# Two fused transformer blocks in fp32 on one core: five changes of order, and a gate projection spread 1, 2, 2, 2 instead of 1, 3, 2, 1

## What is computed

```python
xn = rms_norm(x, norm_gain)
qa, ka, va, za, qi, ki, wi, qb, kb, vb, zb = split(xn @ w_in)     # 8 heads of 64 in each half
a_out = dsa_attention(...)      # an index score picks the 128 keys of each query (top-k), softmax over them
b_out = dilated_attention(...)  # three dilated windows
x = x + concat([a_out * silu(za), b_out * silu(zb)]) @ w_out
...
x = x + hybrid_layer(x, ...)    # second block: compressed, selected and window attention, pooling
x = x + square(relu(rms_norm(x) @ w_ff1)) @ w_ff2
return rms_norm(x)
```

## Time and profile before

| | before |
|---|---|
| median of three runs | 1025.14 us (1024.88 to 1025.60) |
| the profiled execution | 1025.67 us, its span 1023.7 us |
| PE busy | 1007.1 us, 98% of the span |
| DVE, ACT, POOL busy | 66%, 54%, 41% |
| PE clock granted | 0.999 of full |

### The profile page before, as it was taken

How to read it: one execution, slowest core, us unless ns; L and a number is a source line. 1 busy time by engine, 2 the same in 40 slices (tenths; PEclk the granted TensorE clock), 3 DMA queues, 4 the chain that set the end, 5 groups by cost and what they waited for, 6 DMA issues and landing times. The chain is left out here.

```text
span 1023.7 us, 14244 instructions
## 1 busy us (share of the span) xinstructions
PE 1007.1 (98%) x5158; PEld 828.0 (81%) x5158; DVE 678.5 (66%) x1201; ACT 555.2 (54%) x1013; POOL 422.4 (41%) x403
## 2 busy tenths in 40 slices
PE   9999999999999999999999999999999999999997
PEld 7788877778778898878887778888888888888885
DVE  5578898788975256733577879344332225999997
ACT  7455354777862456544667874224443346554555
POOL 0024012666730003900354520007779965774753
PEclk9999999999999999999999999999999999999999
DMA  9533321337140384132200461249999941443552
GB/s 338 104 98 98 98 62 42 83 84 203 46 175 1 122 278 133 46 99 62 63 2 1 156 209 47 83 143 306 361 350 338 349 166 63 153 152 126 209 183 82
DMA packets 100165, 146.24 MB, mean 143 GB/s; under 512 B 6480, under 2 KB 60496, under 8 KB 100096
## 3 DMA queue, kind: packets, MB, share of 16 engines
q1 hardware_dynamic: 86800, 130.75, 39.0%
q10 hardware_dynamic: 12768, 12.88, 4.0%
q0 software_dynamic: 528, 1.70, 1.0%
HBM read 123.69 MB, written 21.63 MB: 142 GB/s over the span
## 5 line engine op out<-in xcount | busy, mean ns | idle before, releaser
L2653 DVE TENSOR_TENSOR w_lo<-wring,w_hi 128x1024 fp32r<-128x1024 f32 x32 | 50.6, 1583 | 108.2 <-ACT w_hi L1997 108.2
L2144 DVE TENSOR_TENSOR u_lo<-wring,u_hi 128x1024 fp32r<-128x1024 f32 (+2 forms) x69 | 83.4, 1215 | 53.2 <-ACT u_hi L1650 52.5
L966 PE MATMUL bank<-u_hi,h_hi 128*128 128x512 f32 (+1 forms) x288 | 110.9, 385 | 0.1
L966 PE MATMUL bank<-u_hi,h_lo 128*128 128x512 f32 (+1 forms) x288 | 109.2, 379 | 0.0
L966 PE MATMUL bank<-u_lo,h_hi 128*128 128x512 f32 (+1 forms) x288 | 109.0, 378 | 0.0
L966 PE MATMUL bank<-h_hi,w_hi 128*128 128x512 f32 (+2 forms) x272 | 103.2, 379 | 0.0
L1650 ACT ACTIVATE u_hi<-wring 128x1024 fp32r<-128x1024 f32 (+1 forms) x64 | 66.2, 1034 | 68.2 <-PE bank L966 51.3
L966 PE MATMUL bank<-h_hi,w_lo 128*128 128x512 f32 (+2 forms) x272 | 103.1, 379 | 0.0
L966 PE MATMUL bank<-h_lo,w_hi 128*128 128x512 f32 (+2 forms) x272 | 103.1, 379 | 0.0
L966 PE MATMUL bank<-h_hi,u_hi 128*128 128x512 f32 x224 | 93.4, 417 | 0.4 <-ACT arena L1592 0.2
L1478 PE MATMUL bank<-s_hi,f_hi 128*128 128x512 f32 x224 | 87.5, 391 | 1.1 <-DVE f_lo L2687 0.9
(11 more groups left out here) (400 smaller groups left out, 2598.8 us busy)
## 6 DMA issues: line engine op xcount, KB each, us to landing
wring<-in_w_in SPq DMA_DIRECT2D x60, 512.0 KB, 3.9
wring<-in_w_ff ACTq DMA_DIRECT2D x12, 1024.0 KB, 9.0
wring<-sums_kept SPq DMA_DIRECT2D x16, 768.0 KB, 4.2
wring<-in_w_ff SPq DMA_DIRECT2D x22, 512.0 KB, 6.6
wring<-in_w_ff SPq DMA_DIRECT2D x32, 256.0 KB, 3.3
sums_kept<-wring SPq DMA_DIRECT2D x22, 256.0 KB, 5.1
wring<-in_w_out SPq DMA_DIRECT2D x2, 2048.0 KB, 13.0
wring<-in_w_ff SPq DMA_DIRECT2D x4, 1024.0 KB, 6.9
```

The lines of the kernel that those rows point to most:

```text
L966: last = mm(b, lhs, rhs, start=(start and n == 0), stop=(stop and n == 2))
L2144: done = v.tensor_tensor(u_lo[raw_place(u)][:, cols], raw_unit(u)[:, cols], u_hi[hi_place(u)][:, cols].bitcast(F32), ALU.subtract)
L2653: v.tensor_tensor(cut(w_lo[ring3(m)]), src, cut(w_hi[ring3(m)]).bitcast(F32), ALU.subtract).then_inc(w_lo_done, 1)
```

## The change

Six edits, none of which adds or removes an instruction.

```diff
-    FILL_STEPS = 4 * ((0, 2, 2, 3, 4, 5, 6),) + 3 * ((0, 1, 2, 2, 3, 3, 4, 5, 6, 7),) + ((0, 1, 2, 2, 3, 3),)
+    FILL_STEPS = 4 * ((0, 2, 3, 4, 5, 6, 7),) + 3 * ((0, 1, 2, 2, 3, 3, 4, 5, 6, 7),) + ((0, 1, 2, 2, 3, 3),)
...
@@ tensor: the held products
                 for t in range(2):
                     second_of(m, 0, t)
+                if m > held[0]:
+                    second_of(held[0], 1, m - held[1])
...
             for q in (1, 2):
                 for t in range(2):
-                    for m in held:
+                    for m in held[1 if q == 1 else 0:]:
                         last = second_of(m, q, t)
...
@@ scalar: after the attention loop
-            mixed_high(7, slice(0, S // 2))
             for m in (8, 9):
                 wo_high(m)
+            mixed_high(7, slice(0, S // 2))
             low_rows_of(GROUPS - 1)
...
@@ vector: projections
                 for k in range(3):
-                    if g != "va":
-                        low(unit_of[(g, k)] + HI_UNITS)
                     if done is not None and k > 0:
                         head_low(done, 2 * k - 2)
                         head_low(done, 2 * k - 1)
+                    if g != "va":
+                        low(unit_of[(g, k)] + HI_UNITS)
                     search(counts[k + 1])
...
@@ vector: attention loop
+            def gate_work(t):
+                if t in MIX_LOW_AT:
+                    mixed_low(MIX_LOW_AT[t])
+                if t in GATED_LATE:
+                    gated(FILL1[GATED_LATE[t]])
...
-                if t == NS + 2:
-                    collect1(GROUPS - 2)
...
-                if t in MIX_LOW_AT:
-                    mixed_low(MIX_LOW_AT[t])
-                if t in GATED_LATE:
-                    gated(FILL1[GATED_LATE[t]])
+                if t < NS - 2:
+                    gate_work(t)
...
+                if t == NS - 2:
+                    gate_work(t)
                 if t == NS:
                     mix(6)
+            collect1(GROUPS - 2)
             mix(7, slice(0, S // 2))
```

## The result

| | before | changed |
|---|---|---|
| median of 22 runs each, same chip | 1025.34 us (1024.72 to 1025.97) | 1026.43 us (1025.31 to 1030.30) |
| ratio | | 1.0016, 95% interval 1.0010 to 1.0022 |
| the profiled execution | 1025.67 us, span 1023.7 us | 1025.31 us, span 1023.3 us |

The changed kernel is slower by 1.1 us, 0.16%. The forecast was 1022.7 us, with a range up to 1024.9: the time lies 1.5 us above the range. The slowdown is smaller than the 0.2% that the prediction took as the least that can be told, but the interval of this timing leaves out 1. Rival 1 (every stall pays) is furthest off.

What follows compares the result with a forecast made beforehand. PE was taken as the bound, busy 1007.1 of 1023.7 us, so gains lay in single waits. Terms 1.5 + 0 + 0.9 + 0 = 2.4 us off 1025.14 gave 1022.7 us, range 1020.5 to 1024.9.

Steps and rivals of the forecast that it cites:

- Rival 1: Every stall removed pays, the tail's 1.1 and 140's 0.8 us on top: 1020.8 us; chance 15%.
- spread of the chunks: First four head pairs: moving a gate chunk from iteration 2 to 6 removes 2.3 us of waits, adds 0.5 and 0.3.
- head_low ahead of low: PE's 0.64 us stall at 140 goes, gaining 0.8 us, but PE waits 0.8 us longer at va: gain 0.
- steps 62 to 66, wo_high: At 283 to 297 us both edits give 1.5 us, of which 0.9 survives the weight units' DMA-anchored chain at 308.
- held products: At 1005 us two products fill PE's 0.94 us stall; PE ends 1.4 us sooner, but DVE sets the end: gain 0.
- sign that the prediction named for being right: No idle at head pair starts or 140, waits near step 4, va and L1015, POOL scaling 0.7 us, PE ending 1.4 earlier.
- I take 0.3 us of new wait: Head pair 3: PE would arrive at 211.4, DVE's score of step 27 end at 211.6 to 212.0, costing 0.3 us.
- Rival 2: The spread only shifts waits, as iteration 4 of each pair becomes the place to wait: 1024.2 us; chance 20%.
- A backlog ... holds the same instructions in either order: DVE's top-k rounds from 128.1 us delay head_sum regardless of the edit, so PE still waits at va.
- to make it up: From 102 to 128 us DVE's 3.1 us idle would absorb about 0.4 us lost in each of four slots.
- moves up only 0.5 us (0.8 less 0.3): Step 63's last transpose, behind which SP issues the weight DMAs, comes 0.5 us sooner after late reciprocals cost 0.3.
- keeps its wait for `f_lo`: In the tail, the banks of q = 0 that start DVE's chain stay unmoved, so the held products gain 0.

Runs made afterwards that it cites:

- The three timings: The changed kernel timed three times against the kernel before: 1026.43 beside 1025.34 us, 1026.07 beside 1025.60, 1026.41 beside 1025.25.
- the third profile: Profile from the third timing of the unaltered changed kernel, whose median was 1026.41 us beside 1025.25 of before, ratio 1.0010.
- the version that beats both: Kernel before with spread in head pairs 1 to 3, low parts first, head_low in qa, one search round moved, 62-66 and wo_high edits, no held products: 1023.00 us, 0.9980.
- the moved round: Changed kernel with one top-k search round moved from the last slot of qa to the first of va: PE 1.4 us better than the changed kernel at 152.
- the last version: The 1023.00 us version with late_half ahead of collect1 and mix, product 12's high part earlier, one unit low part ahead of DVE's first addition: 1022.71 us, ratio 0.9980.
- the repeats: The kernel before, unchanged, executed three more times for its profile: all end 0.72 to 0.75 us sooner behind 998 than its first profile.
- the kernel with the pair first: Kernel before with the spread, and DVE making steps 18 and 19's low part first in iteration 22: PE gains 0.18 us from 152 to 222; execution 1029.06 us.

## Why the prediction was wrong, by its steps

| term | forecast, us gained | measured | where |
|---|---|---|---|
| spread of the chunks | 1.5 (0 to 2.3) | -0.22 to -0.27 | head pair 3 gives all back |
| head_low ahead of low | 0 (up to 0.8) | -0.24 to -0.31 | collision at 97 and 102 |
| steps 62 to 66, wo_high | 0.9 (0.45 to 1.5) | +0.31 to -0.66 | units asked for no sooner, and landing late |
| held products | 0 (0 to 1.1) | -0.38, or 0 in the slower pattern | q = 0 comes later |
| sum | 2.4 | -0.5 to -1.6 | -0.22 -0.24 +0.31 -0.38, -0.27 -0.31 -0.66 -0.38 |

The three timings, -1.09, -0.47 and -1.16 us, lie in or at the edge of the last line. The profiles come out lower than two of the timings: from 50 us to the end of the span the changed kernel's three took 0.55 us more in the mean than the four of before.

Nearly every sign that the prediction named for being right was seen: no wait before L1119 at the starts of head pairs and 0.43 us at a step 4, none at 140 and 1.11 at va, POOL's scaling in 0.66 us, PE's last product ending 1.5 us before DVE's last add. The wait at L1015 stood where the earlier trace rows has these transposes, not at 304 to 305, and only the third profile shows it as idle time (0.96 us). The signs told whether the waits aimed at would go, and none of them looked for a new one in head pair 3 or at the transposes of step 63. (Two thirds of 0.60 and 0.15 are 0.55, not 0.57.)

**The spread: the step that failed is "I take 0.3 us of new wait" in head pair 3, and the 0.5 of gain behind it.** Of the waits named, those of 179.59 and 192.98 went as forecast, and the one at step 4 of head pair 0 came with 0.44 us where 0.5 was said. The one of 220.41 went too, where PE came 0.2 us later. Head pairs 1 and 2 gained 0.77, where the prediction's waits add up to 0.97. But the wait of 0.35 us at 209.16, which was to go, grew to 1.07. I had looked at the scores of step 27 for the new wait and not at what stands on DVE ahead of the low part in iteration 22, and I took DVE's durations as fixed. The wait at step 28 itself was sized too small as well (0.63 us in the version that beats both), but in the changed kernel, where PE waits 1.07 us at 209 ahead of it, it doesn't show. Rival 2 (the spread only shifts waits) was right for this term, and named step 4 where the larger new wait is the one for `pt_pair_lo`.

**head_low: the zero was right as absorption and wrong as a bound.** "A backlog ... holds the same instructions in either order" is what the moved round confirms. The step that failed is that DVE has 3.1 us idle from 102 to 128 "to make it up". Of these, 0.73 lie ahead of the `u_lo` of 102.73, 1.3 behind 124, and the 1.1 between are DVE's own small steps: what is lost at 102 reaches `head_sum` in full. What is lost is another thing than the 0.4 us per slot, namely 0.25 us from two instructions that take longer beside each other.

**Steps 62 to 66.** POOL's step took 0.66 us as forecast, and the stall at 285.5 went, where held durations had given 0.25; so the same mechanism that I used here for a gain I left out in the other two places. PE was 0.5 us ahead at 291, where 0.9 was said, and 1.25 at 296, where 1.6 was (by the terms ahead of the last one). The step that failed is "moves up only 0.5 us (0.8 less 0.3)", for the last transpose of step 63: it moved up by nothing. POOL's scaling of step 63 ended at 285.55 + 1.51 = 287.06 in before, 0.4 us ahead of PE; the "some 0.5 us later" of the reciprocals puts it past 287.48, where PE started, so PE could gain nothing there, and the prediction booked a loss of 0.3 of the 0.8 instead of all. With the issue of the units unmoved only the slack at 308 can be kept. That slack of 0.45 is 0.42 by the third profile, in which PE starts 0.06 us behind the row, and about 0.30 with what a wait costs beyond its idle time: the 0.3 us that was kept in two of the changed kernel's profiles. The third lost it, and more, to units that landed 1 us later. "About 0.1 us is lost" at 297, which is 0.7, failed as well but counts for little: 0.54 us was left when PE came to 308, still more than the slack, and in the last version, with 0.91 us left, 0.55 were lost there.

**Held products.** That the start of the chain "keeps its wait for `f_lo`" is the step that failed. Six matmuls of 0.23 us are 1.38, and in the pattern that fifteen of eighteen profiles show PE has only 0.97 us to put them in (read in the kernel with the spread alone); the rest stands ahead of the banks that the chain begins with. In the pattern of the profile that was read, the forecast holds: the same two products cost nothing there. What went wrong is that one execution's pattern was taken for the kernel's, and that six matmuls were not compared with the wait at all: 1.38 beside the 0.94 us of the earlier trace rows would have shown that the zero hangs on what else PE waits for.

**The price of a wait.** The prediction took 0.16 us beyond the idle figure. At 1005.04 in before it is 0.17 on the matmul that waited and 0.11 on the next, 0.28 in all.

**The baseline.** The sum was made against one profile that stood 0.53 us above its median. Its last products ran in the slower of two patterns, 0.73 us longer; the repeats show the other. That, and a start 0.43 us sooner, is why the changed kernel's own profile looked faster.

**POOL beside DVE.** Row against row, both take longer when DVE's instruction reads two operands in SBUF: `u_lo` 1.77 us beside and 0.68 apart, POOL's product 1.72 and 1.30, its four low parts 5.64 and 5.39, its scaling 1.61 and 0.66. `pt_pair_lo`, which reads PSUM, kept its 0.68 in each place. The Trainium skill (GPSIMD Engine Reference, Specifications) names DVE instructions with two SBUF inputs as ones that contend with GpSimd. The traces agree, by the rows just named.

## What to carry to other kernels

An edit that lets an engine run earlier shifts what runs beside what: look up which DVE instruction with two SBUF operands meets which POOL instruction at the new times, and price the longer one, on the engine that is waited for. Ask of each stall that goes whether the next instruction that waits for another engine, and the next transfer, move up too: if they don't, the gain ends there. Work moved into a stall must be shorter than the stall in every pattern that the executions show, or it delays what the stall was for. For changes of a microsecond, compare the streams of one engine instruction by instruction, over several executions, and take off what differs ahead of the first edit.

## What was not expected of the hardware

The first 26 us differ from execution to execution: PE's stream stands at -0.45 to +0.21 us in the four profiles of before, at -0.43 to +0.24 in the three of the changed kernel, and at -0.6 to +2.9 us in all eighteen. The latest one is the kernel with the pair first, PE:

```profile
23.17 1.03 PE L1058 MATMUL bank<-arena 32*16 32x512 f32 x2 [0.64 <-DMA arena<-in_rel_bias]
...
25.32 1.79 PE L1065 MATMUL bank<-arena 128*128 128x128 f32 x8 [0.91 <-DVE arena L2197]
```

and the same kernel's stretches, us, then busy us (count) of PE, PEld, DVE, ACT, POOL, PE's clock, DMA share, GB/s:

```profile
22.00:25.60 3.60, 2.05 (x9) 0.64 (x8) 1.48 (x6) 2.99 (x7) 0.00 (x0) 1.00 0.79 285
25.60:29.10 3.50, 3.50 (x14) 3.03 (x13) 3.11 (x8) 3.45 (x6) 0.79 (x1) 0.51 0.02 8
```

A table landed late and PE waited for it, waited again for DVE behind it, so that it was busy 2.05 of 3.60 us, and then had the lower of its two clock levels, 1.2 GHz, for 3.4 us, where its products start 0.43 us apart instead of 0.23. Of the 2.9 us, 1.3 were lost when the row of 25.32 starts (24.02 in before), and 1.6 behind that, with the clock. In no other profile did the clock fall before PE had finished.

This execution took 1029.06 us and is the only one over 1028 us that was profiled. Whether the others, of 1028 us and more, are of this kind is not shown. They are not spread evenly: 7 of 44 timed executions of the changed kernel and 1 of 12 of it without the held products, but 2 of 98 of before (1030.48 and 1028.40) and none of 54 of the spread alone, all but the spread, the held products alone and the last two versions. So the changed kernel may well have a cause of its own for them, which no run here shows. A branch's weights near 612 us add 0 to 0.9 us in some executions, of before too.

The last products run in one of two patterns of DVE and POOL. Of eighteen profiles three have the slower one (that of before, the round moved, the last version), with three different kernels; what picks it is open. Open too is how much of the first timing's 1.09 us belongs to the landing of the units: it depends on how often they come late, and the three profiles of the changed kernel show 0.02, 0.03 and 0.99 us. The first and the third timing are 0.5 and 0.6 us above the 0.55 by which the profiles differ in the mean, and what makes that up is not shown.
